# The second feed-forward product by seven products of quarters, its weight sums on GpSimd

## What is computed

```python
def swiglu(x, w13, w2):
    a, b = jnp.split(x @ w13, 2, axis=-1)
    return (jax.nn.silu(a) * b) @ w2

def ffn_half_step(h, g, shift, scale, gate, w13, w2):
    return h + 0.5 * gate * swiglu(modulate(rms_norm_2(h, g), shift, scale), w13, w2)
```

## Time and profile before

| | |
|---|---|
| time, median of 3 runs | 4195.26 us |
| lowest and highest | 4182.81, 4198.72 us |
| profiled execution's span | 4193.0 us |
| its own time beside the span | not listed apart; the span is taken for it |
| TensorE busy | 3991.0 us (95%) |
| VectorE busy | 2480.2 us (59%) |
| ScalarE busy | 1708.2 us (41%) |
| GpSimd busy | 202.8 us (5%) |
| 768-token stages, first to last matmul | 1710.9 to 2221, 2545.4 to 3056, 3067.9 to 3579 us |

### The profile page before, as it was taken

One profiled execution on the slowest core, in us unless ns is written; L12 is line 12 of the kernel. 1 busy time (PEld: TensorE's weight loads), 2 busy tenths in 40 slices (PEclk: granted clock), 3 DMA queues, 4 the chain that ended last, 5 costly groups with the idle time before them and its releaser, 6 DMA issues. The chain is left out here.

```text
span 4193.0 us, 92837 instructions
## 1 busy us (share of the span) xinstructions
PE 3991.0 (95%) x40800; PEld 3568.4 (85%) x40800; DVE 2480.2 (59%) x3882; ACT 1708.2 (41%) x2992; POOL 202.8 (5%) x159
## 2 busy tenths in 40 slices
PE   6999999998999998999999999999999999989999
PEld 5777777777788887999997769999999999668998
DVE  5565665554444443756655557566576665657776
ACT  4433433342255554533333425333353333445443
POOL 0111111011000000000001110000000000120000
PEclk9999999999999999999999999999999999999999
DMA  4001010004345545112121101211212112112222
GB/s 172 19 14 28 28 28 27 27 4 160 126 170 180 180 177 220 61 71 71 61 81 54 59 31 61 72 70 61 81 53 74 65 61 81 64 58 73 105 106 81
DMA packets 99875, 337.03 MB, mean 80 GB/s; under 512 B 5009, under 2 KB 66834, under 8 KB 71826
## 3 DMA queue, kind: packets, MB, share of 16 engines
q1 hardware_dynamic: 99474, 331.09, 22.1%
HBM read 326.62 MB, written 4.46 MB: 79 GB/s over the span
## 5 line engine op out<-in xcount | busy, mean ns | idle before, releaser
L1042 PE MATMUL banks<-x_hi,w_hi 128*128 128x384 f32 (+1 forms) x2496 | 806.7, 323 | 12.6 <-ACT ffn_tiles L1172 6.3
L1043 PE MATMUL banks<-x_lo,w_hi 128*128 128x384 f32 (+1 forms) x2496 | 802.6, 322 | 0.0
L1044 PE MATMUL banks<-x_hi,w_lo 128*128 128x384 f32 (+1 forms) x2496 | 802.6, 322 | 0.0
L1149 ACT CAST w_hi<-landing_all 128x512 fp32r<-128x512 f32 x768 | 457.4, 619 | 317.0 <-DVE landing_all L1254 300.2
L1246 DVE TENSOR_TENSOR w_lo<-landing_all,w_hi 128x512 fp32r<-128x512 f32 x768 | 515.6, 684 | 49.9 <-ACT w_hi L1149 49.8
L1042 PEld LDWEIGHTS banks<-x_hi,w_hi 128*128 128x128 f32 x2496 | 471.6, 189 | 21.9 <-DVE x_lo L1352 9.5
L1043 PEld LDWEIGHTS banks<-x_lo,w_hi 128*128 128x128 f32 x2496 | 471.9, 189 | 0.4
L1044 PEld LDWEIGHTS banks<-x_hi,w_lo 128*128 128x128 f32 x2496 | 471.8, 189 | 0.0
L1043 PE MATMUL banks<-g_lo,w_hi 128*128 128x384 f32 (+1 forms) x1234 | 421.7, 342 | 0.0
L1042 PE MATMUL banks<-g_hi,w_hi 128*128 128x384 f32 (+1 forms) x1234 | 421.6, 342 | 0.0
L1044 PE MATMUL banks<-g_hi,w_lo 128*128 128x384 f32 (+1 forms) x1234 | 421.6, 342 | 0.0
(11 more groups left out here) (491 smaller groups left out, 7514.3 us busy)
## 6 DMA issues: line engine op xcount, KB each, us to landing
landing_all<-in_w SPq DMA_DIRECT2D x132, 1024.0 KB, 4.8
arena_first<-in_ada_w SPq DMA_DIRECT2D x38, 2048.0 KB, 8.6
weight_ring_first<-in_rw_pair SPq DMA_DIRECT2D x32, 512.0 KB, 5.2
landing_all<-in_w_in SPq DMA_DIRECT2D x12, 1024.0 KB, 4.8
weight_ring_first<-in_da_head SPq DMA_DIRECT2D x16, 512.0 KB, 9.7
weight_ring_first<-in_da_head SPq DMA_DIRECT2D x8, 1024.0 KB, 6.3
landing_all<-in_w_out SPq DMA_DIRECT2D x8, 1024.0 KB, 5.2
x_normed_first<-in_ada_w SPq DMA_DIRECT2D x3, 2048.0 KB, 10.9
```

Source lines behind the costliest of these rows:

```text
L1042: mm(o, wh, xh, start=first, stop=False, skip_group_check=onto)
L1043: mm(o, wh, xl, start=False, stop=False, skip_group_check=onto)
L1044: return mm(o, wl, xh, start=False, stop=last, skip_group_check=onto)
L1149: nc.scalar.copy(SH[:, q % RING], raw(q)).then_inc(whi.h, 1)
```

## The change

The three 768-token stages call a new function, `ffn_sevens`; the 512-token stage keeps `ffn`. What differs:

- The second product of w0 to w4 is made by seven products of quarters too. Its two loads each hold two output row blocks by two depth halves, and each load is 7 slots. A product in a slot makes two banks (ab = 0, 1) of 384 columns with two triples each, 12 matmuls, as a slot of the first product has. The eight residual adds of 768 columns for a group of four tiles become one add per product and bank: 28, each 384 columns (for the second token half in two instructions of 128 and 256 columns).
- The sums of weights of these loads are made by GpSimd, in place in the landing buffer, each after a low part. Those of the first product stay with VectorE.
- The hidden tiles are handled in pairs. Their quarters are cast and split, four chained sums of g are made in place by VectorE, then cast (1536 columns) and split.
- The ring of weight slots has 8 places instead of 11, and no slot is split early at the start. The g buffers become 7 x 2 quarters of 384 columns, and four raw tiles are kept instead of two.
- Banks are given out by a small planner. w5 uses 512 and 256 columns in place of twice 384. The packed second weights are laid out in quarters by the host.

```diff
+        PLAIN, RING, RAW = 2, 8, 4
+        bank_of = (0, 1, 2, 0, 0, 0, 2)
+        target = ((0, 0), (0, 0), (1, 1), (1, 1), (1, 0), (0, 1), (1, 0))
+        w_order = (P1, P2, P6, P5, P7, P3, P4)
...
+            elif u < 5:
+                order += [q + P1] + held + [q + p for p in w_order[1:]] + [q + 7 + p for p in w_order]
+                held = []
...
+                def second(q):
+
+                    _, c, part, _, q0 = slots[q]
+                    first, x, r = part in (P1, P2, P5), g_operand[part], q % RING
+                    pe.wait_ge(glo.h, glo.at(0, 4 * c + (3 if part in (P1, P2, P4) else 4)))
+                    pe.wait_ge(wlo.h, wlo.at(0, q + 1))
+                    for ab in range(2):
+                        b = bank_at(q, ab)
+                        if first:
+                            take_bank(b, out_done, out_no[q0 + {P1: P4, P2: P2, P5: P3}[part], ab])
+                        else:
+                            pe.wait_ge(out_done.h, out_done.at(0, out_no[q0 + {P6: P1, P7: P6, P4: P7, P3: P5}[part], ab]))
+                        for k in range(2):
+                            ins = triple(bank(b), SH[:, r, 2 * ab + k], SL[:, r, 2 * ab + k], OH[:, x, k], OL[:, x, k], k == 0 and first, k == 1, not first)
+                        ins.then_inc((first_done if ab == 0 else slot_done).h, 1)
...
+            @block.gpsimd
+            def _(pool):
+                for q0, s in sevens.items():
+                    if slots[q0][0] == "g":
+                        continue
+                    b11, b12, b21, b22 = quarters(q0)
+                    pool.wait_ge(wlo.h, wlo.at(0, q0 + P1 + 1))
+                    nc.gpsimd.tensor_tensor(b11, b12, b11, ALU.subtract).then_inc(wsum.h, 1)
+                    pool.wait_ge(wlo.h, wlo.at(0, q0 + P2 + 1))
+                    pool.wait_ge(wsum.h, wsum.at(0, 4 * s + 1))
+                    nc.gpsimd.tensor_tensor(b12, b22, b12, ALU.subtract).then_inc(wsum.h, 1)
+                    pool.wait_ge(wlo.h, wlo.at(0, q0 + P5 + 1))
+                    pool.wait_ge(wsum.h, wsum.at(0, 4 * s + 2))
+                    nc.gpsimd.tensor_tensor(b11, b22, b11, ALU.subtract).then_inc(wsum.h, 1)
+                    pool.wait_ge(wlo.h, wlo.at(0, q0 + P7 + 1))
+                    pool.wait_ge(wsum.h, wsum.at(0, 4 * s + 3))
+                    nc.gpsimd.tensor_tensor(b21, b21, b11, ALU.subtract).then_inc(wsum.h, 1)
+                norm.add_first(pool)
...
+                def split(q):
+                    _, _, part, n, q0 = slots[q]
+                    made = {P5: 1, P7: 2, P6: 3, P4: 4}.get(part, 0) if q0 in sevens else 0
+                    if made:
+                        act.wait_ge(wsum.h, wsum.at(0, 4 * sevens[q0] + made))
...
+                def g_sums_high(u):
+                    act.wait_ge(g_sums.h, g_sums.at(0, u // 2 + 1))
+                    nc.scalar.copy(OH[:, GS2:GS1 + 1, u % 4 // 2], raw_pair(u)).then_inc(ghi.h, 1)
...
+                def g_sum(u):
+                    g = raw_pair(u)
+                    dve.wait_ge(glo.h, glo.at(0, u))
+                    L(tt(g[:, 3], g[:, 1], g[:, 3], ALU.add))
+                    L(tt(g[:, 1], g[:, 0], g[:, 1], ALU.subtract))
+                    L(tt(g[:, 0], g[:, 3], g[:, 0], ALU.subtract))
+                    tt(g[:, 2], g[:, 2], g[:, 0], ALU.subtract).then_inc(g_sums.h, 1)
...
+                def add_out(q, ab):
+                    _, _, part, n, q0 = slots[q]
+                    x, h = target[part]
+                    x, at = x + 4 * loads[n][2] + 2 * ab, 512 * bank_at(q, ab) - h * H
+                    if part in (P2, P7, P3):
+                        dve.wait_ge(out_done.h, out_done.at(0, out_no[q0 + {P2: P1, P7: P5, P3: P6}[part], ab]))
+                    for c, c0, cn in in_half[h]:
+                        xs = X[:, x, c0:c0 + cn]
+                        ins = stt(xs, PS[:, at + c0:at + c0 + cn], half[:, x, c:c + 1], xs, ALU.mult, ALU.add)
+                    ins.then_inc(out_done.h, 1)
...
+                    elif kind == "w":
+                        dve.wait_ge(first_done.h, first_done.at(0, product_no[q] + 1))
+                        add_out(q, 0)
+                        done()
+                        add_out(q, 1)
...
+                    if n - 2 in pair_end:
+                        g_low(pair_end[n - 2])
+                    if pair_end.get(n - 3, FT) < FT - 1:
+                        g_sum(pair_end[n - 3])
+                    if pair_end.get(n - 5, FT) < FT - 1:
+                        g_sums_low(pair_end[n - 5])
...
+                    if n:
+                        for q in splits_at[n - 1]:
+                            split(q)
...
-            K.ffn(layer, 1, BOTH, m, gain("g_ffn1"), f"{layer}_1", mix_first(layer))
+            K.ffn_sevens(layer, 1, m, gain("g_ffn1"), f"{layer}_1", mix_first(layer))
...
+            if last:
+                K.ffn(layer, 2, LATENT, lambda j: m(j + 6), gain("g_ffn2"), f"{layer}_2", [])
+            else:
+                K.ffn_sevens(layer, 2, lambda j: m(j + 6), gain("g_ffn2"), f"{layer}_2", ffn_first(1, layer + 1))
```

More of the change, by code:

```diff
@@ L251 @@
     "k_rstd_wide": "heads_copied",
+    "first_product_done": "tr_done",
+    "g_sums_made": "xz_done",
 }
@@ L3706, in build @@
             gain = lambda n: K.par(n)[:, 8 * layer:8 * layer + 8]
-            K.ffn(layer, 1, BOTH, m, gain("g_ffn1"), f"{layer}_1", mix_first(layer))
+            K.ffn_sevens(layer, 1, m, gain("g_ffn1"), f"{layer}_1", mix_first(layer))
             K.mix_buffers(f"mix{layer}")
             K.mixing(layer, last, gain("g_mix"), m(3), m(4), m(5), ffn_first(2, layer))
-            K.ffn(layer, 2, segs, lambda j: m(j + 6), gain("g_ffn2"), f"{layer}_2", [] if last else ffn_first(1, layer + 1))
+            if last:
+                K.ffn(layer, 2, LATENT, lambda j: m(j + 6), gain("g_ffn2"), f"{layer}_2", [])
+            else:
+                K.ffn_sevens(layer, 2, lambda j: m(j + 6), gain("g_ffn2"), f"{layer}_2", ffn_first(1, layer + 1))
         K.final(K.par("g_final"))
@@ L3754, in packed @@
         w2 = a[f"w2_ffn{n}_2"].reshape(DEPTH, FT, P, KT, P)
-        fours = w2[:, 0:20].reshape(DEPTH, 5, 4, P, 2, 4, P).transpose(0, 1, 4, 3, 5, 2, 6).reshape(DEPTH, 10, P, 2048)
+        fours = w2[:, 0:20].reshape(DEPTH, 5, 2, 2, P, 2, 2, 2, P).transpose(0, 1, 5, 4, 3, 7, 6, 2, 8).reshape(DEPTH, 10, P, 2048).copy()
+        if n == 2:
+            fours[DEPTH - 1] = w2[DEPTH - 1, 0:20].reshape(5, 4, P, 2, 4, P).transpose(0, 3, 2, 4, 1, 5).reshape(10, P, 2048)
         two = w2[:, 20:22].transpose(0, 2, 3, 1, 4).reshape(DEPTH, 1, P, 2048)
```

443 lines of the change are left out of this document (added).

## The result

The changed kernel takes 4206.28 us in the median of 20 runs (4198.43 to 4222.48), the kernel before, again over 20 runs, 4192.79 us. The ratio is 1.0035, 95% interval 1.0026 to 1.0044: slower by 0.35%. I forecast 4188 us, 0.2% faster. The time lies inside the range, but it went the other way. One execution among all those of the test kernels (of the one with one-column sums) took 7460.6 us and is not explained; that kernel's median hardly depends on it.

A forecast was written before the change was run, and what follows sets the result against it. TensorE's matmuls were taken to set the time. Per stage, -20.8 us of matmuls plus 18.3 (waits 14.3, start 3.4, collisions 0.6) gave -2.5, three stages -7.5: 4188 us, range 4158 to 4226.

The forecast's parts named there:

- What is removed: Second product of the 768-token stages: 120 fewer matmuls a stage at 0.1732 us, 20.8 us, 62.4 us over three stages.
- The shorter ring: Weight ring of 8: P6 comes 3 slots after release; TensorE waits 0.51 us per P6, 0.96 or 0.36 at some units.
- Repacked weights, transfers, banks, the 512 and 256 columns: Second-product loads, bank reuse and last tile pair: each put at nothing, banks unless VectorE falls behind.
- VectorE is busy: Sign that the forecast is right: VectorE busy over 80% of a steady stretch.
- GpSimd's sums: Second-product weight sums beside VectorE: 40 a stage, small price of 0.6 us a stage.
- The rival on the slower side: Second product: GpSimd sums hold VectorE's low parts beyond 2.0 us slack a load; 4203 to 4281 us, chance 0.23.
- the start: Start of a 768-token stage, early splits gone: TensorE starts P6 at 1754.8 instead of 1751.4, 3.4 us.
- The clock behind the pause: TensorE behind its waits: a lower granted clock would void the sum; no term given.
- collisions: VectorE operations stretched beside GpSimd's sums: 0.6 us a stage in the sum.
- Rival 1: P6 waits absent, only the stage start costs: 4145 us, or 4166 with half the waits; chance 0.2.

## Why the prediction was wrong

**Right.** What is removed: exactly 360 matmuls, 62 us at their spacing. The shorter ring: P6 waits where the working put them and by its three sizes, 0.51 as 0.56, 0.96 as 1.02, 0.36 as 0.32; the first 0.05 is in the hand-over, 0.37 us by the earlier trace rows and 0.42 here. P6 of g2 starts 3.46 us later than before, counted from the stage's first matmul, in the first stage and 3.47 in the third; 3.4 was forecast. Repacked weights, transfers, banks, the 512 and 256 columns: no wait of their own. VectorE is busy 354 of 430 us between 1760 and 2190, 82%.

**Wrong, first: GpSimd's sums.** The step says: "A sum starts at the end of a low part and lasts 1.3 us; VectorE's next work is an add from a bank". At the step in which P3 ends it isn't: behind the add come the two gatings, with both operands in SBUF. I had written of such operations that they stretch beside GpSimd, and looked only at the low parts. And this is the one place where VectorE has nothing to spare, the chain in front of P6. It cost 1.2 us at 4 P6 a stage, 14 us, and another 0.4 a stage at w4; 0.6 a stage was put down. The rival on the slower side had the mechanism (a hold), but mostly the wrong place: it counted holds of low parts against a load's slack of 2.0 us. Such holds exist too, but only in w4 (4 low parts a stage, one of them 1.78 us instead of 0.68, the others 0.94 or 0.95); the wait of 0.4 there stands behind the last of them, while the one of 1.78 cost TensorE nothing. One hold on the chain decides, at any slack of the load.

The Trainium skill ("SBUF — State Buffer", Who interferes with whom) has the rule that fits: two SBUF inputs on VectorE against a GpSimd instruction that reads SBUF. The rows agree: 2.23 us for the pair of gatings against 1.02, the neighbour that reads a bank unchanged at 0.56, and 1.02 again with one-column sums. Asked for the gatings and not for the low parts, the rule gives the price as an estimate: the second gating waits for what is left of the fourth sum, 1.22 us (1792.59 to 1793.81); it took 1.08 us longer, and the first one 0.12.

**Wrong, second: the start.** The step stops at TensorE's first matmul of P6: 3.4 us. The clock behind the pause was named only as something that would void the sum, with no term. It cost 1.5 us in the first stage, 2.8 in the second and 2.5 in the third (excess in the slots P6 and P5 of g2 beyond the pause, less the 0.1 of before): 6.8 us.

The sum: 14.5 for the gatings, 1.3 at w4 less the 1.8 put down for collisions, 6.8 for the clock and 2 at the other P6 (the 0.05 and 0.06, less the 0.04 at four units) make 23 of the 25 us by which the three stages together missed (-7.5 forecast, +17.7 measured). What is left is of the size of the spacings under 0.21 us behind each wait, which the table doesn't count.

**Rival 1** (no waits at P6) didn't happen; that the wait of each unit of the first product was right to 0.07 us shows that the order lists, read by hand, are worth the work. **Not tested:** a ring of 9 or 10 with the seven products; by the order lists they would release P6 four and five slots ahead instead of three. Whether SBUF has the room is open.

## What to carry to other kernels

Where an order is written out by hand, list for each buffer slot when it is released, when it is read, and what stands in the producing engine's queue between. If a chain in front of the bottleneck engine is as long as its slack, the order of two operations in it can be worth as much as the change's arithmetic: here 35 us by moving one operation, where 62 us of matmuls were saved. Work handed to GpSimd is not free beside VectorE: look for VectorE operations with two SBUF operands on the critical chain, and keep them away from it or make them read PSUM. And a ring that gets shorter to make room is part of the change's price: measure it alone (with the early splits dropped beside it, 42 of the 62 us here).

## What the runs showed of the hardware that was not expected

A pause of TensorE of 1.4 us left the granted clock at 1.00; one of 3.5 us was followed by 0.50 to 0.58 in stretches of 2 us and by matmuls 0.32 us apart, in all three stages of the changed kernel. But the length of the pause alone doesn't tell. Five of the kernels have this pause of 3.5 us, 15 times in all; behind 14 of them come slow matmuls (7 to 17 spacings of 0.32 us), and behind one, in the second stage of the kernel with the low part first, none:
```profile
2578.00:2580.00 2.00, 0.17 (x1) 0.00 (x0) 2.00 (x2) 0.91 (x3) 0.00 (x0) 1.00 0.00 0
2580.00:2582.00 2.00, 0.33 (x2) 0.36 (x3) 1.97 (x5) 1.98 (x4) 0.00 (x0) 1.00 0.00 0
2582.00:2584.00 2.00, 2.00 (x13) 2.00 (x12) 2.00 (x4) 0.10 (x1) 0.00 (x0) 1.00 0.02 4
...
2581.67 0.41 PE L1549 MATMUL banks<-x_hi,w_hi 128*128 128x384 f32 x1 [3.50 <-DVE w_lo L1780]
```
With all sums on VectorE, pauses of 1.8 us at w0 to w3 were followed by 0.32 us spacing in 3 of 12 places and those of 2.1 us at w4 in all three, while pauses of 2.1 us in the kernel that also has the low part first left it at 0.173 each time. What decides is open.

GpSimd's 128x512 sum took 1.29 us undisturbed, 1.68 behind a low part of VectorE that was still running, and 1.41 behind the first gating; VectorE's pair of gatings was held for 1.2 us. In all 12 places of the three stages these durations are the same to 0.01 us, and each time the one of the two that started later is the one stretched: the gating that starts 0.19 us behind the fourth sum ends 0.4 us after it, and in w4 a low part that starts 0.06 us behind a sum of 1.29 us takes 1.78 us.
